# Attention's 32-row block exchange: DMAs replaced by VectorE copies

## The reference

```python
def one_block(qi):                       # 128 queries, 4 heads
    s = jnp.einsum('bqhd,bkhd->bhqk', qi, k).astype(jnp.float32) * scale
    p = jax.nn.softmax(s, axis=-1).astype(v.dtype)
    return jnp.einsum('bhqk,bkhd->bqhd', p, v)
# prompt tokens: 256 keys; sample tokens: 512 cached + 1024 own = 1536 keys
```

## Time and profile before

| | |
|---|---|
| device time, median of 3 runs | 2403.8 us (2402.75 to 2405.05) |
| the profiled execution: device time | 2406.11 us |
| the profiled execution: span, first to last instruction | 2404.4 us |
| outside the span | 1.7 us |
| mean granted TensorE clock | 0.978 of full |
| HBM read / written | 339.34 MB / 47.65 MB |

### The profile page before, as it was taken

One profiled execution on the slowest core, in us unless ns is written; L12 is line 12 of the kernel. 1 busy time (PEld: TensorE's weight loads), 2 busy tenths in 40 slices (PEclk: granted clock), 3 DMA queues, 4 the chain that ended last, 5 costly groups with the idle time before them and its releaser, 6 DMA issues.

```text
span 2404.4 us, 30025 instructions
## 1 busy us (share of the span) xinstructions
PE 2282.0 (95%) x12052; PEld 1488.4 (62%) x12052; DVE 785.3 (33%) x1444; ACT 514.0 (21%) x1050; POOL 490.9 (20%) x685
## 2 busy tenths in 40 slices
PE   6999999999997999999989999899999959999996
PEld 4545555655444888788755455455654447887884
DVE  2401155553328211121143022555623552211213
ACT  2310032222334110001142001222323320110012
POOL 3000023342001332232210000243310022322321
PEclk9999999999998999999999999999999979999998
DMA  9100066875455898899950002754342268998888
GB/s 340 36 0 22 19 176 162 168 159 132 149 188 212 265 285 284 281 287 292 324 181 18 22 1 88 165 125 106 93 123 97 87 217 282 287 292 279 281 289 301
DMA packets 205114, 427.61 MB, mean 178 GB/s; under 512 B 29312, under 2 KB 64312, under 8 KB 205024
## 3 DMA queue, kind: packets, MB, share of 16 engines
q1 hardware_dynamic: 162336, 352.28, 44.8%
q0 software_dynamic: 24832, 55.61, 10.1%
q10 hardware_dynamic: 17856, 18.49, 3.3%
HBM read 339.34 MB, written 47.65 MB: 161 GB/s over the span
## 4 chain that ended last, share of the span: by engine, by line
PE 88%; DMA 4%; DVE 3%; SPq 3%; issue 1%; ACT 1%; ACTq 0%; POOL 0%; DVEq 0%; POOLq 0%
PE PS L1430 11%; PE PS L1268 11%; PE PS L1437 11%; PE PS L1459 9%; PE PS L1049 9%; PE PS L1200 7%; PE PS L1142 6%; PE PS L1003 6%; PE PS L990 4%; PE PS L1154 3%; PE PS L1453 2%; PE PS L1103 1%; DMA r<-r 1%; DMA ring<-in_w_down_dram 1%; PE PS L1288 1%
## 5 line engine op out<-in xcount | busy, mean ns | idle before, releaser
L1430 PEld LDWEIGHTS PS<-r,ring 128*128 128x128 f32 x2048 | 285.8, 192 | 25.9 <-issue 24.0
L1430 PE MATMUL PS<-r,ring 128*128 128x160 f32 x2048 | 288.1, 302 | 10.8 <-ACT r L1751 9.6
L1268 PE MATMUL PS<-ring,mix 128*128 128x512 f32 x640 | 287.8, 597 | 0.0
L1437 PE MATMUL PS<-r,ring 128*128 128x160 f32 x2048 | 283.4, 299 | 0.0
L1437 PEld LDWEIGHTS PS<-r,ring 128*128 128x128 f32 x2048 | 279.9, 190 | 0.0
L1459 PE MATMUL PS<-ring,r 128*128 128x512 f32 x496 | 221.2, 599 | 0.0
L1049 PE MATMUL PS<-r,ring 128*128 128x512 f32 (+1 forms) x576 | 208.4, 521 | 1.6 <-ACT r L1551 1.6
L1268 PEld LDWEIGHTS PS<-ring,mix 128*128 128x128 f32 x640 | 116.9, 190 | 128.1 <-issue 127.9
L1142 PE MATMUL PS<-lat,r 128*128 128x512 f32 (+1 forms) x416 | 188.6, 588 | 4.0 <-ACT r L1594 2.7
L1200 PE MATMUL PS<-r 128*128 128x256 f32 x768 | 176.2, 387 | 13.6 <-issue 13.6
L1200 PEld LDWEIGHTS PS<-r 128*128 128x128 f32 x768 | 148.8, 194 | 49.2 <-issue 29.5
(11 more groups left out here) (309 smaller groups left out, 2343.2 us busy)
## 6 DMA issues: line engine op xcount, KB each, us to landing
ring<-in_w_gate_dram SPq DMA_DIRECT2D x32, 2048.0 KB
ring<-in_w_up_dram SPq DMA_DIRECT2D x32, 2048.0 KB
ring<-in_w_down_dram SPq DMA_DIRECT2D x31, 2048.0 KB
ring<-in_w_ada_dram SPq DMA_DIRECT2D x15, 2048.0 KB, 11.3
r<-ring SPq DMA_DIRECT2D x108, 96.0 KB
x_dram<-r SPq DMA_DIRECT2D x20, 512.0 KB, 2.9
r<-x_dram SPq DMA_DIRECT2D x20, 512.0 KB, 4.5
r<-r SPq DMA_DIRECT2D x96, 96.0 KB
```

What stands on the lines that cost most here:

```text
L1268: ins = pe.matmul(psum(2 * (s % 2) + n, 512), mix[:, k, tile * P:(tile + 1) * P], W_OUT[n][:, k, :], start=(k == 4), stop=(k == 3))
L1430: ins = pe.matmul(PS[:, b // 2, (b % 2) * 256:(b % 2) * 256 + SLOTS], W_G[:, k, b * P:(b + 1) * P], XST[par][:, k, :], start=(k == 0), sto ...
L1437: ins = pe.matmul(PS[:, 2 + b // 2, (b % 2) * 256:(b % 2) * 256 + SLOTS], W_U[:, k, b * P:(b + 1) * P], XST[par][:, k, :], start=(k == 0), ...
```

## The change

All twelve blocks whose quarter changes are now copied by DVE; POOL keeps the four others, and the exchange has no DMAs. A new `move_blocks(n)` stands in DVE's stream behind `invert_sums(n)` and ahead of `bias_modulation`. `pt_kept` now counts 16 an item from both engines, and the semaphores `pt_landed` are gone. The `exchange` of SP and of ACT (the same function, with `act` for `sp`) is removed, with its calls. In the diff the changed waits stand in the order SP, POOL, PE, ACT, DVE. POOL's `keep_diagonal(n)` has one more wait: until all 16 blocks of item n - 1 are copied.

```diff
+MOVES = 16
-        pt_landed = [sem(f"pt_landed{i}") for i in range(2)]
...
-                def exchange(n, quarters):
-
-                    groups, x = groups_of(n)
-                    sp.wait_ge(p_turned, at(l, 2 * NI, 2 * n + 2))
-                    if n >= 2:
-                        sp.wait_ge(o_summed, at(l, NI, n - 1))
-                    for a in quarters:
-                        for b in [b for b in range(4) if b != a]:
...
-                            sp.dma_start(dst[:, :, x * b:x * (b + 1)], src[:, :, x * a:x * (a + 1)])\
-                                .then_inc(pt_landed[n % 2], 16)
...
-                    exchange(n, (0, 1) if n < NI - 1 else range(4))
...
-                sp.wait_ge(pt_landed[0], at(l, 192 * NI // 2, 192 * NI // 2))
-                sp.wait_ge(pt_kept, at(l, 4 * NI, 4 * (NI - 1)))
+                sp.wait_ge(pt_kept, at(l, MOVES * NI, MOVES * (NI - 1)))
...
                     if n == 0:
                         pool.wait_ge(ada_zeroed, l + 2)
+                    else:
+                        pool.wait_ge(pt_kept, at(l, MOVES * NI, MOVES * n))
...
-                        pe.wait_ge(pt_landed[n % 2], at(l, 192 * NI // 2, 192 * (n // 2 + 1)))
-                        pe.wait_ge(pt_kept, at(l, 4 * NI, 4 * (n + 1)))
+                        pe.wait_ge(pt_kept, at(l, MOVES * NI, MOVES * (n + 1)))
...
-                        act.wait_ge(pt_landed[n % 2], at(l, 192 * NI // 2, 192 * (n // 2)))
-                        act.wait_ge(pt_kept, at(l, 4 * NI, 4 * (n - 1)))
+                        act.wait_ge(pt_kept, at(l, MOVES * NI, MOVES * (n - 1)))
...
-                    if n < NI - 1:
-                        exchange(n, (2, 3))
...
+                def move_blocks(n, quarters):
+
+                    groups, x = groups_of(n)
+                    dve.wait_ge(p_turned, at(l, 2 * NI, 2 * n + 2))
+                    if n:
+                        dve.wait_ge(pt_kept, at(l, MOVES * NI, MOVES * n))
+                    if n >= 2:
+                        dve.wait_ge(o_summed, at(l, NI, n - 1))
+                    for a in quarters:
+                        for b in [b for b in range(4) if b != a]:
+                            dst = turned(n)[32 * a:32 * a + 32, 0:4 * groups * x].rearrange("p (g x) -> p g x", g=groups)
+                            src = Pr[n % 2][32 * b:32 * b + 32, 0:4 * groups * x].rearrange("p (g x) -> p g x", g=groups)
+                            dve.tensor_copy(dst[:, :, x * b:x * (b + 1)], src[:, :, x * a:x * (a + 1)]).then_inc(pt_kept, 1)
 ...
                     divide_out(n - 4)
                     invert_sums(n)
+                    move_blocks(n, (0, 1, 2, 3))
                     bias_modulation(chunk_at(l, n))
```

More of the change, by code:

```diff
@@ L552, in load_ada_bias @@
                             .then_inc(ada_landed[i % 2], 16)
-                def exchange(n, quarters):
-                    groups, x = groups_of(n)
-                    sp.wait_ge(p_turned, at(l, 2 * NI, 2 * n + 2))
-                    if n >= 2:
-                        sp.wait_ge(o_summed, at(l, NI, n - 1))
-                    for a in quarters:
-                        for b in [b for b in range(4) if b != a]:
-                            dst = turned(n)[32 * a:32 * a + 32, 0:4 * groups * x].rearrange("p (g x) -> p g x", g=groups)
-                            src = Pr[n % 2][32 * b:32 * b + 32, 0:4 * groups * x].rearrange("p (g x) -> p g x", g=groups)
-                            sp.dma_start(dst[:, :, x * b:x * (b + 1)], src[:, :, x * a:x * (a + 1)])\
-                                .then_inc(pt_landed[n % 2], 16)
                 for i in range(2):
@@ L792, in _ @@
                 keep_diagonal(NI - 1)
-                pool.wait_ge(pt_kept, at(l, 4 * NI, 4 * NI))
+                pool.wait_ge(pt_kept, at(l, MOVES * NI, MOVES * NI))
                 spread_inverses(NI - 1)
@@ L1640, in copy_value_heads @@
                     act.activation(mix[:, h, t0:t0 + 512], psum(bank, 512), ACT.Copy).then_inc(uvh_copied[0], 1)
[L1642 to L1653, removed]
                 for n in range(NI):
```

## The result

| | before | after |
|---|---|---|
| median of 4 runs, same chip | 2404.43 us (2402.75 to 2406.31) | 2552.31 us (2550.10 to 2555.43) |
| profiled execution (span) | 2406.11 us (2404.4) | 2551.69 us (2550.0) |
| mean granted clock | 0.978 | 0.957 |

The ratio is 1.0616 (95% interval 1.0597 to 1.0634): 147.9 us slower by the medians, 145.6 by the profiled executions. Forecast were +163.7 and 2567 us.

A forecast was written before the change was run, and what follows sets the result against it. PE's matmuls bound attention until the moves make DVE the bound. Plain items 92.4, chunk items 57.6, items 2 and 3 13.8, prompt 20.8 and 4, gaps -17.9, tail -7: +163.7, so 2567 us; 8 in 10 range 2460 to 2625.

The forecast's parts named there:

- What bounds: Attention: PE's matmuls set 13.30 us an item, DVE has 5.56 us of room; with the moves DVE becomes the bound.
- Price of a copy: DVE in attention: each 32 x 768 copy takes 0.58 us, twelve 7.0 us an item (ends 5.4 and 11.5).
- Full overlap: Rival for DVE's moves: copies overlap and no collision, 5.4 us an item, +32, 2436 us; chance 0.09.
- half the pace: Rival for DVE's moves: 0.97 us a copy, 11.6 an item, +218, 2622 us; chance 0.11, with the collision 0.04.
- Collision with POOL: Attention: POOL's four diagonal copies fall together with DVE's moves, 0.7 us each, 2.8 us an item (ends 0 and 3.5).
- Chunk items: Attention items with a chunk: moves ahead of the bias delay PE's turn and rotary scores, 22.7 against 15.5, +7.2 us each.
- prompt items, 4 (clock included): Four prompt items in attention: copies of 256 and collision cost 5.2 us each, 20.8, plus 1 each for the clock.
- items 2 and 3, 4: Early attention items: their old period was 3.45 us shorter, with only a prompt item's `times_values` in them; 13.8 extra.
- full-length items without, 20, the gaps taken off: Attention items without a chunk: +4.2 us each as DVE bounds; vanishing gaps give -17.9 us.
- around and behind attention: Behind each layer's last item: PE waits for the last exponentials only, -3.5 us a layer, -7 in all.
- The gaps: PE in attention: three gaps, 13.0 us, and slow matmuls behind them, 4.9, vanish as POOL's wait shrinks; gain 17.9 us.
- Added waits: DVE's waits on `p_turned`, `pt_kept` and `o_summed`, and POOL's on DVE's copies of n - 1, cost nothing.

The follow-up runs named there:

- six copies: Kernel after with the bias ahead of the moves, POOL's copies behind them, and only quarters 0 and 1 moved, the other six blocks left out: 2427.22 us, 1.0034.
- the late read-back: Kernel before, all DMAs kept, with POOL's read-back of the inverses of item n - 1 put behind the diagonal copies of item n: 2390.36 us, 0.9884.

## Why the prediction was right

**What bounds.** Right. The argument "DVE has 7.74 us of work in 13.30 and gets more than the remaining 5.56" decided the sign, and holds at both ends: with six copies PE bounds, with twelve DVE does. PE was forecast near 75% busy and was at 80 and 84.

**Price of a copy.** Right: 0.58 forecast, 6.97/12 = 0.58 clear of POOL, against 0.553 for the length of one. "Full overlap" and "half the pace" fall.

**Collision with POOL.** The mechanism is right, the size was not: 0.5 per copy of POOL instead of 0.7, so 2.0 instead of 2.8 an item. The 0.7 came from divisions with two inputs and their own lengths. POOL pays as well: its four copies take 4.16 us instead of the 3.46 that they take clear of DVE's copies. The Trainium skill, "SBUF — State Buffer", section "Who interferes with whom", states that GpSimd and a VectorE instruction that is in a two-port mode, or has two SBUF inputs, shut each other out for a whole instruction. That both bursts grow agrees; no row shows in which mode the copies, which have one input, ran.

**Chunk items.** Right in place, cause and size. For the six of full length +7.2 was forecast and +7.2 to +7.6 measured: the collision is 0.8 smaller and the stretch from bias to maximum 5.75 instead of 5.2. What was missed is the item behind a chunk, 17.6 to 18.0 instead of 16.7: its second scores are late, and its two maxima have 0.8 to 1.1 us of idle time between them.

**The terms.** By the starts of the first maxima:

| | forecast | measured |
|---|---|---|
| prompt items, 4 (clock included) | +24.8 | +16.3 |
| items 2 and 3, 4 | +36.6 | +26.3 |
| full-length items with a chunk, 6 | +43.2 | +44.3 |
| full-length items without, 20, the gaps taken off | +66.1 | +57.2 |
| around and behind attention | -7.0 | +1.5 |
| sum | +163.7 | +145.6 |

So the term that was mis-sized is the collision: 0.8 too much in 22 plain items is 17.6 us, of which the items behind chunks give some back. In the prompt and in items 2 and 3 there was often none at all, because POOL was late: the dozen that starts at 357.32 in layer 0 takes 6.97. Copies of 256 elements took 0.28 to 0.33. That the sum came within 18 us is in part luck: the first, second and fourth terms were 28 too high together, and the last was 8.5 too low, with the wrong sign.

The last term had the wrong sign. I took it that only the exponentials hold PE at the end of a layer's attention. PE after, and before, behind the first maximum of the last item:

```profile
1879.41 1.02 PE L1200 MATMUL PS<-mix,ring 128*128 128x512 f32 x2
1886.76 6.94 PE L1200 MATMUL PS<-mix,ring 128*128 128x512 f32 x10 [6.34 <-DVE mix L1985]
```

```profile
1742.62 5.43 PE L1214 MATMUL PS<-mix,ring 128*128 128x512 f32 x12
```

The projections of heads wait for a division which DVE does behind both maxima and the turn. From the first maximum (1879.03 and 1734.88) to this matmul it is 7.73 us after and 7.74 before: nothing is gained.

**The gaps.** That they vanish was right, by the wrong reason. "POOL's wait shrinks" hardly holds: 296.9 to 283.8 us, while two executions of the kernel before differ as much (296.9 and 308.8). They vanished because the exponentials now wait for DVE alone, which comes later than POOL. With the DMAs kept, the late read-back removes POOL's share of them, and in its profiled execution 8.2 us are left behind the DMAs.

**Added waits.** "Nothing" is right for the kernel as measured, and wrong as a general statement: with the bias first and POOL behind, DVE waited 19.7 us for POOL's diagonals, with six moves 41.2 in layer 0 alone. The largest single extra that was avoidable is two lines in the wrong order on DVE: 74 us, of which by estimate 19 are collisions that fell away with it.

**Left open.** Why the round trip of an inverse store takes some 8 to 9 us with or without the exchange's transfers, and why the kernel before had 13.0 us of gaps in the first profile and 25.6 in the later one, no run here tells.

## What to carry to other kernels

Before work is moved onto an in-order engine, compare it with that engine's free time in one period of the bound (here 5.56 us, 9.6 copies), not with its share of the whole span: a DVE that was busy for a third of the time became the bound. Put it behind whatever another engine waits for (here the bias), split what doesn't fit over engines that are idle in the same period, and count the other engine's work beside it as a cost.
When a gap disappears with a large change, try its supposed cause alone: one wait moved in POOL's list was worth 1.2% by itself, and its trace showed what the cause did not cover.

## What the runs showed of the hardware that was not expected

- A POOL copy of 32x768 fp32 cost DVE's stream of copies 0.5 us, and took itself 1.04 instead of 0.86.
- Copies of 32x768 that change their quarter follow at 0.58 us; within a quarter some 0.1 less where the rows are those of the copy before.
- An ACT copy of 32x768 took 0.84 us, 0.29 more than DVE's, and six an item were fully hidden.
- POOL waited some 8 to 9 us for a small store to DRAM to land, both beside the exchange's twelve transfers an item (8.7) and beside none of them (7.9 and 8.7).
- The same kernel took 2404 us when the result was measured and 2420 to 2422 later, on each of two chips, with PE's waits ahead of `times_values` in attention at 13.0 and 25.6 us; the kernel in which DVE bounds attention took 2552 and 2554.
